# First block's gate stored by itself, layers' vectors turned in front of the latent rows' attention, and three feed-forward norms modulated in rows

## The chip, the cores and the metric

The kernel runs on one core of one Trainium2 chip. The metric is the time of one execution on the device, in microseconds (us). PE is the matrix engine (TensorE), DVE VectorE, ACT ScalarE, POOL GpSimd and SP SyncE, which here only issues the weight loads.

## The reference

A first block and two layers of a second block, on 256 latent tokens and 256 context tokens of width 1024. What the change touches is modulation by vectors that come out of the condition `c`, and the gates:

```python
# first block
x = x + gate2[:, None, :] * y2            # y2: the retrieval of experts ("peer")
return rms_norm(x, final_norm_w)
# second block, per layer l; x: latents, xc: context (not in the last layer)
x = x + gt_a * _rms(y, g_attn_post[l])                       # y: attention output @ w_out
hf = _rms(x, g_ffn_pre[l]) * (1.0 + sc_f) + sh_f
x = x + gt_f * _rms(_swiglu(hf, w_gate, w_up, w_down), g_ffn_post[l])
```

`mod = silu(c) @ w_ada + b_ada` gives the shifts, scales and gates, six vectors of 1024 for each block or layer and stream.

## The kernel before, in words

All engines walk one hand-written list of steps, `PLAN` (`make_plan`), and each emits its part of a step, so that list is the program order on PE, DVE, ACT and POOL alike. `weave(a, b)` mixes two lists by a table of costs. Every engine executes in order, so a wait holds up all that stands behind it on that engine. Streams are named (layer, stream, part): stream 0 is the latents, 1 the context, part "a" the attention and "f" the feed-forward.

Weights come in chunks of 128 x 1024 through a ring: SP loads a chunk into one of four buffers `RAW`, ACT copies its high part into one of three buffers `SPL` (`split_hi`), DVE subtracts to get the low part (`split_lo`), and PE multiplies high and low parts (three products each, `bk<-SPL,HH` and so on). A chunk's `SPL` buffer is free once PE has used it. Tokens' features are held turned (features on partitions) as a high and a low part, `HH`/`HL` for the latents and `HCH`/`HCL` for the context. Rows of `w_ada` ("ada" steps) go through the same ring and are multiplied and summed by DVE (L1189) into columns of `MOD`.

**Vectors.** The modulation vectors are columns (one feature per partition). A gate is applied to rows (tokens on partitions), so it has to lie in rows: step `vt` of layer 0 turns 104 columns of `MOD` (the first block's gate `MOD[:, 40:48]` and the layer's 96) and 64 of `AB` on PE, ACT copies them to `TMP`, POOL stores them to DRAM (`vec`, L738 and L739), and later loads them back, broadcast to all 128 partitions (`row_of`, L747, 512 KB each). In layer 0 the row of the first block's gate (`gB2`) is loaded in the same step `vt`, behind both stores; `vt` stands after the last modulation of layer 0 (`mods 0 f`), just in front of `peer_out`. The step `peer_out` (DVE: eight operations of 128x512) multiplies the four banks of the retrieval's output by that row and adds them to x; then come the final norm and layer 0's latents. Step `gB` loads a layer's gate row once its last attention output is there.

**Loads by POOL.** `c_in` loads x, the context, small rows and the final norm's weight while the first block still runs.

**Norm in front of a feed-forward** (`pre_steps`). `an_b` on DVE updates x (two operations of 128x1024, L1164), ACT squares the two halves with a sum. `norm_k` (DVE, L1161) makes the mean, POOL raises it to the power -1/2 (L680), `norm_b` on DVE refines it by three small operations and multiplies the rows by it (two L1159). `nT` then turns eight blocks of 128x128 for each half i of the tokens on PE (L1786), in two steps of four. For the first four of a half ACT applies scale and shift as per-partition vectors (4 operations), for the others DVE (4 operations, L1161); ACT makes the high part of the half (128x1024), DVE the low part (two of 128x1024 at the end). The first matmul of the feed-forward waits for all of it. For (0, 1, f) and for (1, 0, f) these steps stand alone in the list; those of (0, 0, f) are woven into the context's feed-forward (0, 1), whose output step `fo` (four operations 128x512 on DVE, four squares on ACT) stands between the last two turnings.

PE's results lie in eight banks, taken in rotations; `take` waits until the bank's former content is read.

## Time and profile before

| | |
|---|---|
| runs | 2423.24, 2421.45, 2420.80 us; median 2421.45 |
| the profiled execution, its own time | 2421.29 us |
| its span, first to last instruction | 2419.2 us |
| busy: PE / DVE / ACT / POOL | 2189.0 / 1721.2 / 1145.4 / 59.6 us |
| mean granted TensorE clock | 0.955 of full speed |

The span leaves 2.1 us of the execution's time outside. In a timeline a line gives the start in us, the length, the engine, the source line, the operation with what it writes and reads; `x4` means four instructions in a row, and `[9.51 <-DMA ...]` means that the engine stood idle for 9.51 us before it and what ended the wait. Many lines of the source are helpers: L1155 is any two-input operation of DVE, L798 and L800 any activation, L1780 any matmul, L1786 any turning.

### The profile page before, as it was taken

The numbers are of one execution on the slowest core, as the hardware profiler recorded it, in microseconds if no ns is written. First come the engines' busy times: TensorE is split into PE (matmuls) and PEld (weight loads), VectorE is DVE, ScalarE is ACT, GpSimd is POOL, SyncE is SP. The second block draws the span as 40 slices with busy tenths as digits, with TensorE's granted clock in tenths as the row PEclk, the third lists the DMA queues.
The fourth block names the chain that finished last, engine by engine and source line by source line (L and its number), as shares of the span: only waits on it lengthen the run. The fifth ranks groups of instructions, "written<-read, shape, count | busy, mean of one in ns | idle before, by whom it ended". The sixth has DMA issues, their size and how long they took to land.

```text
span 2419.2 us, 37731 instructions
## 1 busy us (share of the span) xinstructions
PE 2189.0 (90%) x14570; PEld 1954.7 (81%) x14570; DVE 1721.2 (71%) x3370; ACT 1145.4 (47%) x1945; POOL 59.6 (2%) x76
## 2 busy tenths in 40 slices
PE   3998799999999999989977989799989988997998
PEld 2987799999987778879855666799979978667997
DVE  5667678889987777788845676577776665665554
ACT  2643344555554444454444445444454445454444
POOL 1000000000000000000001000000000000000000
PEclk9999999999999999999978999899999999898999
DMA  8648646664467877777731120477767763104664
GB/s 283 199 145 275 202 145 197 200 219 136 149 193 259 274 258 247 272 230 246 258 102 40 54 69 18 133 242 250 244 208 254 253 192 120 60 1 123 187 187 131
DMA packets 139120, 438.80 MB, mean 181 GB/s; under 512 B 15553, under 2 KB 38369, under 8 KB 138432
## 3 DMA queue, kind: packets, MB, share of 16 engines
q1 hardware_dynamic: 109440, 396.93, 51.5%
q10 hardware_dynamic: 25776, 23.97, 2.9%
q0 software_dynamic: 3728, 15.50, 1.8%
q8 instruction: 117, 1.92, 0.3%
q14 instruction: 59, 0.48, 0.1%
HBM read 422.58 MB, written 13.76 MB: 180 GB/s over the span
## 4 chain that ended last, share of the span: by engine, by line
PE 49%; DVE 13%; issue 10%; DMA 10%; ACT 5%; POOL 0%; ACTq 0%; DVEq 0%; POOLq 0%; SPq 0%
PE bk L1780 46%; DMA TMP<-kept 4%; DVE SPL L1155 4%; DMA RAW<-in_peer 3%; PE bk L1786 3%; ACT SPL L798 2%; DMA kept<-TMP 1%; DVE RAW L1189 1%; ACT R L800 1%; DVE R L1155 1%; DVE TMP L1155 1%; DVE ST L1170 1%; ACT R L798 1%; DVE R L1164 1%; DVE WHL L1155 1%
## 5 line engine op out<-in xcount | busy, mean ns | idle before, releaser
L1155 DVE TENSOR_TENSOR SPL<-RAW,SPL 128x1024 fp32r<-128x1024 f32 (+1 forms) x614 | 744.2, 1218 | 352.0 <-ACT SPL L798 350.6
L798 ACT ACTIVATE SPL<-RAW 128x1024 fp32r<-128x1024 f32 (+1 forms) x614 | 645.1, 1054 | 615.0 <-PE bk L1780 284.2
L1780 PE MATMUL bk<-HH,SPL 128*128 128x256 f32 x3840 | 748.6, 289 | 28.2 <-DVE HL L1155 13.7
L1780 PEld LDWEIGHTS bk<-HH,SPL 128*128 128x128 f32 x3840 | 622.4, 194 | 35.1 <-DVE HL L1155 14.3
L1780 PE MATMUL bk<-SPL,WHL 128*128 128x512 f32 x2328 | 553.8, 391 | 13.4 <-DVE WHL L1155 9.2
L1780 PE MATMUL bk<-HL,SPL 128*128 128x256 f32 x1920 | 547.9, 285 | 0.0
L1780 PEld LDWEIGHTS bk<-SPL,WHL 128*128 128x128 f32 x2328 | 428.5, 188 | 106.5 <-issue 19.2
L1780 PEld LDWEIGHTS bk<-HL,SPL 128*128 128x128 f32 x1920 | 373.4, 194 | 2.5
L1780 PE MATMUL bk<-SPL,HH 128*128 128x256 f32 (+1 forms) x1664 | 314.0, 291 | 31.4 <-DVE SPL L1155 19.4
L1780 PEld LDWEIGHTS bk<-SPL,HH 128*128 128x128 f32 x1664 | 267.4, 198 | 41.1 <-issue 24.3
L798 ACT ACTIVATE R<-bk 128x256 f32<-128x256 f32 (+4 forms) x350 | 169.1, 498 | 222.2 <-PE bk L1780 197.0
L1780 PE MATMUL bk<-R 128*64 128x256 f32 (+8 forms) x944 | 246.3, 410 | 24.9 <-ACT R L798 11.6
L1780 PE MATMUL bk<-SPL,HL 128*128 128x256 f32 (+1 forms) x832 | 239.7, 288 | 0.0
L1780 PEld LDWEIGHTS bk<-R 128*64 128x64 f32 (+5 forms) x944 | 137.2, 178 | 98.7 <-issue 36.8
L1189 DVE CUSTOM_DVE_ANT_0 RAW<-RAW,TMP 128x1024 f32<-128x1024 f32 x144 | 174.8, 1221 | 14.5 <-ACT TMP L798 7.6
L1780 PEld LDWEIGHTS bk<-SPL,HL 128*128 128x128 f32 x832 | 164.5, 198 | 0.0
L1786 PE MATMUL bk<-cons,R 128*128 128x128 f32 (+1 forms) x626 | 106.1, 305 | 57.9 <-DVE R L1159 23.0
L1786 PEld LDWEIGHTS bk<-cons,R 128*128 128x128 f32 (+1 forms) x626 | 78.2, 153 | 96.3 <-issue 35.6
L800 ACT ACTIVATE R<-bk,ST 128x512 f32<-128x512 f32 (+1 forms) x120 | 74.0, 617 | 140.6 <-DVE ST L1159 139.6
L1780 PE MATMUL bk<-HCH,SPL 128*128 128x256 f32 x704 | 131.1, 285 | 6.7 <-DVE HCL L1155 4.5
L1780 PEld LDWEIGHTS bk<-HCH,SPL 128*128 128x128 f32 x704 | 112.3, 194 | 8.0 <-DVE HCL L1155 4.9
L1170 DVE TENSOR_REDUCE ST<-bk 128x1 f32<-128x512 f32 (+1 forms) x120 | 71.9, 599 | 54.1 <-PE bk L1780 53.9
(136 smaller groups left out, 1940.8 us busy)
## 6 DMA issues: line engine op xcount, KB each, us to landing
RAW<-in_peer SPq DMA_DIRECT2D x256, 512.0 KB, 4.7
RAW<-in_ada SPq DMA_DIRECT2D x144, 512.0 KB, 4.8
RAW<-in_ffn SPq DMA_DIRECT2D x132, 512.0 KB, 4.3
RAW<-in_win SPq DMA_DIRECT2D x96, 512.0 KB, 4.7
RAW<-in_ffd SPq DMA_DIRECT2D x66, 512.0 KB, 4.3
RAW<-in_wout SPq DMA_DIRECT2D x32, 512.0 KB, 5.0
kept<-TMP ACTq DMA_DIRECT2D x88, 128.0 KB, 3.3
TMP<-kept ACTq DMA_DIRECT2D x66, 128.0 KB, 5.6
```

Source lines behind the costliest of these rows:

```text
L798: ins = e.activation(out, in_, func, bias=bias, scale=scale)
L800: ins = e.activation(out, in_, func, bias=bias, scale=scale, accum_out=accum)
L1155: e.tensor_tensor(out, a, b, op).then_inc(*dve.up(*points))
L1164: e.scalar_tensor_tensor(out=out, in0=a, scalar=s, in1=b, op0=op0, op1=op1).then_inc(*dve.up(*points))
L1170: e.tensor_reduce(out, a, AX.X, op).then_inc(*dve.up(*points))
L1189: e.tensor_tensor_reduce(out=raw(n) if last else spare[n in in_ext], in0=raw(n), in1=c, scale=1.0, scalar=0.0, op0=ALU.mult, op1=ALU.add, ...
L1780: ins = e.matmul(out, lhsT, rhs, start=start, stop=stop, skip_group_check=True)
L1786: ins = e.transpose(b[0:rows, n * P:(n + 1) * P], a, ident)
```

## The change

It has three parts.

1. The first block's gate gets a step of its own, `("vt", "peer")`: 8 columns are turned, copied and stored right after `gB1`, before the first block's output projection. Its row is loaded at the head of `c_in` instead of behind layer 0's stores.
2. The steps `vt` of layers 0 and 1 stand in front of the latents' attention rows (units of the differential heads first) instead of at the end of the stage before. Layer 0's now turns 96 columns of `MOD`.
3. The norms (0, 0, f), (0, 1, f) and (1, 0, f) apply scale and shift in rows. `gB` of part "a" loads two more rows, A = (1 + scale) * weight and B = shift. `norm_k` multiplies x by A (two operations 128x1024, the first ahead of the wait for the sum of squares), `norm_b` makes x * r + B (two L1164-type operations in place of two L1159). `nT` then only copies each four turned blocks as high part (ACT, 128x512) and subtracts (DVE, 128x512). The squares' unused output goes to another buffer.

```diff
@@ -266,7 +266,7 @@
-    plan += fill + [("merge", 0), ("merge", 1)] + [("gB1", h) for h in range(2)]
+    plan += fill + [("merge", 0), ("merge", 1)] + [("gB1", h) for h in range(2)] + [("vt", "peer")]
@@ -316,7 +316,7 @@
-    peer += late + [("mods", 0, "f"), ("vt", 0)]
+    peer += late + [("mods", 0, "f")]
@@ -324,11 +324,11 @@
-    plan += weave(others, rows[:mla]) + weave(heads, rows[mla:gqa]) + rows[gqa:-16] + [("sil2", 1)] + rows[-16:]
+    plan += [("vt", 0)] + weave(others, rows[:mla]) + weave(heads, rows[mla:gqa]) + rows[gqa:-16] + [("sil2", 1)] + rows[-16:]
-    ffn = weave(ffn_steps(0, 0)[:-3], last[24:]) + [("mods", 1, "f"), ("vt", 1)]
+    ffn = weave(ffn_steps(0, 0)[:-3], last[24:]) + [("mods", 1, "f")]
@@ -336,7 +336,7 @@
-    plan += weave(others, rows[:mla]) + weave(heads, rows[mla:gqa]) + rows[gqa:]
+    plan += [("vt", 1)] + weave(others, rows[:mla]) + weave(heads, rows[mla:gqa]) + rows[gqa:]
@@ -425,13 +425,15 @@
-        turned_mod = {0: MOD[:, 40:144], 1: MOD[:, 144:192]}
+        ROWNORM = {(0, 0, "f"): 17088, (0, 1, "f"): 13188, (1, 0, "f"): 17088}
+        turned_mod = {"peer": MOD[:, 40:48], 0: MOD[:, 48:144], 1: MOD[:, 144:192]}
+        vec_at = {"peer": TMP[:, 1024:1152], 0: TMP[:, 2560:2688], 1: TMP[:, 2560:2688]}
-        VECS = {"peer": (0, 0)}
+        VECS = {"peer": (1, 160)}
-                VECS[(l, s, "f", "A")], VECS[(l, s, "f", "B")] = (l, 120 + 32 * s), (l, 48 * s + 24 + (0 if l else 8))
+                VECS[(l, s, "f", "A")], VECS[(l, s, "f", "B")] = (l, 120 + 32 * s), (l, 48 * s + 24)
@@ -623,6 +625,9 @@
+        for t, a in ROWNORM.items():
+            NORM[t]["Ar"], NORM[t]["Br"] = R[:, a:a + 1024], R[:, a + 1024:a + 2048]
@@ -694,7 +699,7 @@
-                    pool.wait_ge(T.at("out", ("dT", 0, 0)))
+                    pool.wait_ge(T.at("out", ("dT", 0, 0)), T.at("vm", 0), T.at("vec", 0))
@@ -734,15 +739,17 @@
             def turn_rows(l):
-                n, m = turned_mod[l].shape[1], turned_ab[l].shape[1]
-                e.dma_start(vec_d[l, 0:n, :], TMP[0:n, 2560:2688]).then_inc(*T.up(f"d_mod{l}", 16, [("vm", l)]))
+                n = turned_mod[l].shape[1]
+                if l == "peer":
+                    e.dma_start(vec_d[1, 160:168, :], vec_at[l][0:n, :]).then_inc(*T.up("d_peer", 16, [("vec", "peer")]))
+                    return
+                m = turned_ab[l].shape[1]
+                e.dma_start(vec_d[l, 0:n, :], vec_at[l][0:n, :]).then_inc(*T.up(f"d_mod{l}", 16, [("vm", l)]))
-                if l == 0:
-                    row_of("peer", gB2)
             def row_of(key, dst):
-                pool.wait_ge(T.at("vm", l), T.at("vec", l))
+                pool.wait_ge(*[T.at("vec", "peer")] if key == "peer" else [T.at("vm", l), T.at("vec", l)])
@@ -750,9 +757,13 @@
             def gB(l, s, k):
+                if k == "a":
+                    for n in ("A", "B"):
+                        row_of((l, s, "f", n), NORM[(l, s, "f")][n + "r"])
             def c_in():
+                row_of("peer", gB2)
@@ -842,6 +853,9 @@
             def nT(t, i, k):
+                if t in ROWNORM:
+                    turn_hi(("nT", t, i, k), H[n["s"]], i, k)
+                    return
@@ -996,9 +1010,12 @@
             def turn_rows(l):
-                key, n, m = ("vt", l), turned_mod[l].shape[1], turned_ab[l].shape[1]
+                key, n = ("vt", l), turned_mod[l].shape[1]
-                A(TMP[0:n, 2560:2688], ps(*key)[0:n, 0:P], ACT.Copy)
+                A(vec_at[l][0:n, :], ps(*key)[0:n, 0:P], ACT.Copy, ("out", key))
+                if l == "peer":
+                    return
+                m = turned_ab[l].shape[1]
@@ -1106,7 +1123,7 @@
             def an_b(l, s, k):
-                    A(v2(QS[(l, s)]["oY"], 2)[:, i, :], LX[s][:, i, :], ACT.Square, ("ssn", l, s, k),
+                    A(v2(QS[(l, s)]["junk"], 2)[:, i, :], LX[s][:, i, :], ACT.Square, ("ssn", l, s, k),
@@ -1201,11 +1218,11 @@
-            def turn_lo(key, Hs, i, k):
+            def turn_lo(key, Hs, i, k, *points):
-                   ALU.subtract, ("out", key))
+                   ALU.subtract, ("out", key), *points)
@@ -1292,8 +1309,16 @@
             def norm_k(t):
-                dve.wait_ge(T.at("ssn", l, s, "a") if k == "f" else T.at("ssn", l - 1, s, "f"))
-                mean_eps(ss_of(t)[0], D, "norm", t)
+                before = ("ssn", l, s, "a") if k == "f" else ("ssn", l - 1, s, "f")
+                n = NORM[t]
+                for i in range(2):
+                    if t in ROWNORM:
+                        if i == 0:
+                            dve.wait_ge(T.at("row", t + ("A",)), dve.own)
+                        tt(v2(n["xn"], 2)[:, i, :], n["x3"][:, i, :], n["Ar"], ALU.mult)
+                    if i == 0:
+                        dve.wait_ge(T.at(*before))
+                        mean_eps(ss_of(t)[0], D, "norm", t)
@@ -1302,10 +1327,17 @@
+                    elif t in ROWNORM:
+                        dve.wait_ge(T.at("row", t + ("B",)))
+                        x = v2(n["xn"], 2)[:, i, :]
+                        stt(x, x, r[:, i:i + 1], n["Br"], ALU.mult, ALU.add, ("xn", t, i))
             def nT(t, i, k):
+                if t in ROWNORM:
+                    turn_lo(("nT", t, i, k), H[NORM[t]["s"]], i, k, ("hT", t, i))
+                    return
@@ -1987,7 +2019,11 @@
             def turn_rows(l):
-                b = take(("vt", l), (6, 7))
+                b = take(("vt", l), MIX if l == "peer" else PROJ[(l, 0)])
+                if l == "peer":
+                    pe.wait_ge(T.at("A2"))
+                    e.transpose(b[0:8, 0:P], turned_mod[l], ident).then_inc(*pe.up(("full", ("vt", l))))
+                    return
```

POOL, first place, from the power of a norm just ahead of `c_in`, through `c_in` (`R<-xs` to `R<-in_rows`) and the steps that follow it, to the end of the old step `vt`; before:

```order
24 L680 TENSOR_TENSOR ST<-ST,cons 128x2
25 L676 DMA TMP<-in_rows 128x2048
26 L676 DMA R<-xs 128x2048
27 L676 DMA R<-in_ctx 128x2x1024
28 L676 DMA R<-in_rows 128x640
29 L676 DMA R<-in_rows 128x1024
30 L680 TENSOR_TENSOR ST<-ST,cons 128x2
31 L676 DMA R<-in_wkvb 128x512
32 L676 DMA R<-in_wqb 128x768
33 L738 DMA vec<-TMP 104x128
34 L739 DMA vec<-TMP 64x128
35 L747 DMA R<-vec 128x1024
```

and now:

```order
25 L685 TENSOR_TENSOR ST<-ST,cons 128x2
26 L681 DMA TMP<-in_rows 128x2048
27 L754 DMA R<-vec 128x1024
28 L681 DMA R<-xs 128x2048
29 L681 DMA R<-in_ctx 128x2x1024
30 L681 DMA R<-in_rows 128x640
31 L681 DMA R<-in_rows 128x1024
32 L685 TENSOR_TENSOR ST<-ST,cons 128x2
33 L681 DMA R<-in_wkvb 128x512
34 L681 DMA R<-in_wqb 128x768
35 L685 TENSOR_TENSOR ST<-ST,cons 128x2 x3
36 L685 TENSOR_TENSOR ST<-ST,cons 128x20
```

A row load (`R<-vec`) stands at the head of `c_in`, and the two stores and the load behind `R<-in_wqb` are gone.

POOL, second place, around the output projections of layer 0, before (the two `R<-vec` are the gates of the latents and of the context, in that order):

```order
43 L680 TENSOR_TENSOR ST<-ST,cons 128x20
44 L680 TENSOR_TENSOR ST<-ST,cons 128x8
45 L676 DMA TMP<-in_rows 128x2048
46 L747 DMA R<-vec 128x1024 x2
47 L680 TENSOR_TENSOR ST<-ST,cons 128x2 x2
```

and now, where the order of the six is gate, A and B of the latents, then gate, A and B of the context:

```order
44 L685 TENSOR_TENSOR ST<-ST,cons 128x20
45 L685 TENSOR_TENSOR ST<-ST,cons 128x8
46 L681 DMA TMP<-in_rows 128x2048
47 L754 DMA R<-vec 128x1024 x6
48 L685 TENSOR_TENSOR ST<-ST,cons 128x2 x2
```

The context's gate was the second row load and is the fourth.

DVE, from the update of x in layer 1's attention output to the first split of its feed-forward, before:

```order
2631 L1164 SCALAR_TENSOR_TENSOR R<-R,ST 128x1024 x2
2632 L1161 TENSOR_SCALAR ST<-ST 128x2
2633 L1155 TENSOR_TENSOR ST<-ST 128x2
2634 L1164 SCALAR_TENSOR_TENSOR ST<-ST 128x2 x2
2635 L1159 TENSOR_SCALAR R<-R,ST 128x1024 x2
2636 L1161 TENSOR_SCALAR R<-bk,AB,MOD 128x128 x8
2637 L1155 TENSOR_TENSOR HL<-R,HH 128x8x128 x2
2638 L1155 TENSOR_TENSOR SPL<-RAW,SPL 128x1024 x2
```

and now:

```order
2635 L1181 SCALAR_TENSOR_TENSOR R<-R,ST 128x1024 x2
2636 L1172 TENSOR_TENSOR R<-R 128x1024
2637 L1178 TENSOR_SCALAR ST<-ST 128x2
2638 L1172 TENSOR_TENSOR R<-R 128x1024
2639 L1172 TENSOR_TENSOR ST<-ST 128x2
2640 L1181 SCALAR_TENSOR_TENSOR ST<-ST 128x2 x2
2641 L1181 SCALAR_TENSOR_TENSOR R<-R,ST 128x1024 x2
2642 L1172 TENSOR_TENSOR HL<-bk,HH 128x4x128 x4
2643 L1172 TENSOR_TENSOR SPL<-RAW,SPL 128x1024 x2
```

Two products with a row are new, one on each side of the small operation for the mean; eight operations on 128x128 and two on 128x1024 have become four on 128x512.

## Rows read from the trace of the kernel before

**Rows 1.** The page, part 1: busy time, share of the span and instructions of each engine
```profile
PE 2189.0 (90%) x14570; PEld 1954.7 (81%) x14570; DVE 1721.2 (71%) x3370; ACT 1145.4 (47%) x1945; POOL 59.6 (2%) x76
```

**Rows 2.** Timeline, 1195 to 1232: start, length (us), engine, line, instruction, idle before
```profile
1208.16 2.98 PE L1780 MATMUL bk<-SPL,WHL 128*128 128x512 f32 x12 [1.27 <-DVE WHL L1155]
...
1211.06 0.24 DVE L1155 TENSOR_TENSOR AB<-MOD,cols 128x8 f32<-128x8 f32 x2
...
1220.81 0.69 DVE L1155 TENSOR_TENSOR R<-bk,R 128x512 f32<-128x512 f32 x1 [9.51 <-DMA R<-vec]
...
1216.68 0.57 POOL L747 DMA_DIRECT2D R<-vec  x1 [2.94 <-DMA vec<-TMP]
...
1230.03 1.22 PE L1780 MATMUL bk<-R 32*128 32x256 f32 x2 [4.36 <-ACT R L800]
```

**Rows 3.** Windows: busy time of each engine, granted clock, DMA share, GB/s
```profile
1229.00:1233.00 4.00, 2.97 (x10) 2.32 (x11) 1.89 (x8) 2.60 (x9) 0.00 (x0) 0.50 0.74 247
```

**Rows 4.** Timeline of four engines at the norm of (1, 0), 2203 to 2221
```profile
2206.17 2.48 DVE L1164 SCALAR_TENSOR_TENSOR R<-R,ST 128x1024 f32<-128x1024 f32 x2
...
2209.86 0.17 DVE L1161 TENSOR_SCALAR ST<-ST 128x2 f32<-128x2 f32 x1 [1.22 <-ACT R L800]
...
2210.11 0.70 POOL L680 TENSOR_TENSOR ST<-ST,cons 128x2 f32<-128x2 f32 x1 [4.57 <-DVE ST L1161]
...
2211.43 1.42 DVE L1159 TENSOR_SCALAR R<-R,ST 128x1024 f32<-128x1024 f32 x2
...
2212.24 3.83 PE L1786 MATMUL bk<-cons,R 128*128 128x128 f32 x16 [8.78 <-DVE R L1159]
...
2213.39 1.51 ACT L798 ACTIVATE R<-bk,MOD,AB 128x128 f32<-128x128 f32 x4 [3.56 <-PE bk L1786]
...
2220.56 0.58 PE L1780 MATMUL bk<-HH,SPL 128*128 128x256 f32 x1 [4.49 <-DVE HL L1155]
```

**Rows 5.** View by tile, HH: count, ns min/median/max, first and last start, forms
```profile
L798 ACT ACTIVATE HH<-bk x18: 382/385/599, 270.7 to 2179.3; 128x256 fp32r<-128x256 f32 x12, 128x512 fp32r<-128x512 f32 x6
...
L1155 DVE TENSOR_TENSOR HL<-bk,HH x18: 424/425/693, 271.3 to 2179.7; 128x256 fp32r<-128x256 f32 x12, 128x512 fp32r<-128x512 f32 x6
```

**Rows 6.** Timeline of POOL and DVE, 1270 to 1285 and 1430 to 1440
```profile
1275.27 4.44 POOL L680 TENSOR_TENSOR ST<-ST,cons 128x20 f32<-128x20 f32 x1 [6.77 <-DVE ST L1161]
...
1275.10 2.38 DVE L1155 TENSOR_TENSOR SPL<-RAW,SPL 128x1024 fp32r<-128x1024 f32 x2
...
1433.97 3.53 POOL L680 TENSOR_TENSOR ST<-ST,cons 128x20 f32<-128x20 f32 x1 [13.14 <-DVE ST L1161]
```

**Rows 7.** Timeline of PE, at the context's norm of layer 0
```profile
1562.62 0.58 PE L1780 MATMUL bk<-HCH,SPL 128*128 128x256 f32 x1 [4.49 <-DVE HCL L1155]
```

**Rows 8.** Timeline of PE and DVE at the latent's norm of layer 0, 1764 to 1784
```profile
1774.47 2.48 DVE L1155 TENSOR_TENSOR R<-bk,R 128x512 f32<-128x512 f32 x4
...
1781.38 0.58 PE L1780 MATMUL bk<-HH,SPL 128*128 128x256 f32 x1 [9.19 <-DVE HL L1155]
```

**Rows 9.** Timeline of DVE and PE inside the context's feed-forward
```profile
1725.47 0.42 DVE L1155 TENSOR_TENSOR WHL<-R,WHL 128x256 fp32r<-128x256 f32 x1
...
1728.56 2.88 PE L1780 MATMUL bk<-SPL,WHL 128*128 128x512 f32 x12
```

**Rows 10.** Timeline of ACT, before layer 0's last scaling
```profile
1975.18 0.43 ACT L798 ACTIVATE TMP<-bk 48x128 f32<-48x128 f32 x2 [3.71 <-PE bk L1993]
```

**Rows 11.** View of line 747, the row loads: DMA from issue to landing
```profile
DMA to landing us min/median/max: 3.9/4.0/5.8
```

**Rows 12.** Windows while the context's inputs load (columns as in rows 3)
```profile
1018.00:1022.00 4.00, 4.00 (x28) 3.64 (x27) 1.06 (x2) 1.15 (x2) 0.00 (x0) 1.00 1.02 374
```

**Rows 13.** Timeline of PE, behind those loads
```profile
1028.29 0.36 PE L1780 MATMUL bk<-HH,SPL 128*128 128x256 f32 x1 [2.56 <-DVE SPL L1155]
```

**Rows 14.** Timeline of DVE and PE at the output projections of layer 0
```profile
1522.68 0.69 DVE L1155 TENSOR_TENSOR R<-bk,R 128x512 f32<-128x512 f32 x1 [1.32 <-ACT R L800]
...
1527.37 0.40 PE L1780 MATMUL bk<-SPL,HCH 128*128 128x256 f32 x2
```

## The prediction

> **What bounds the kernel now.** The page's part 1 comes first: PE is busy for 2189 of 2419 us [rows 1], so time is won where PE stands still, and any other engine matters only where PE waits for it. The list of PE's idle gaps then names the places that the change touches. At the end of the first block DVE waits 9.51 us for the gate's row, and PE stands still behind it [rows 2]. In front of three feed-forwards PE waits for the low part of the normed tokens: 4.49 us for (1, 0) [rows 4], 4.49 us for (0, 1) [rows 7], and 9.19 us for (0, 0) [rows 8]. All else in the change moves work between queues, and I read the DMA windows and the rows of POOL and DVE at the new places for what may be late there. The profiled execution is 2421.29 us long, 2.1 us of it outside the span, and the median of the runs is 2421.45; I add the sum to 2421.3.
>
> **1. The gate's own step.** Before, two stores, the wait for them and the load stand behind the last modulation. The load was issued at 1216.68 and DVE went on 4.1 us later [rows 2]. The gate's columns of `MOD` are complete long before, and the new row is loaded in the stretch of [rows 12], some 190 us ahead of its use. DVE's 9.51 us disappear. What is late next: `peer_out` also needs the retrieval's last matmuls, which ended at 1208.16 + 2.98 = 1211.14, and stands behind the AB operations, which end at 1211.30 [rows 2]. So it starts at 1211.3 and not at 1220.8: −9.5. Behind it come the final norm and the first norm of the latents, a chain of latencies with nothing bound to a time of its own, so it moves as a whole.
>
> The clock bears on this. PE has long pauses behind the chain, the last 4.36 us before 1230.03 [rows 2], and the granted clock is 0.50 in 1229 to 1233 [rows 3], the lower level of 1.2 GHz. With DVE's wait gone, these pauses shrink by up to 8 us together; whether what is left of them still lets the clock fall no row shows. PE spent 4 us at half clock there, worth at most 2.0 us. I take half: −1.0 (bounds 0 and −2.0).
>
> **2. The norm of (1, 0).** Followed down the new order, from the update of x, which ends at 2206.17 + 2.48 = 2208.65 [rows 4]. The first product with A is an operation with two inputs of 128x1024; two such take 2.38 us [rows 6], so 1.2 each. It fits into the 1.22 us in which DVE waited for the sum of squares [rows 4]: nothing. The mean ends at 2210.1, then the second product runs until 2211.3 beside POOL's power. Before, the power took 0.70 us and the scaling began at 2211.43. The second product has two inputs from SBUF, and beside such operations POOL's power of 128x20 took 4.44 us where it took 3.53 us alone [rows 6]: 0.91 us more. I take this for the new place, so the power ends at 2211.7, three small operations of DVE add 0.6 to 0.7, and the first x * r + B ends at 2212.4 + 1.24 = 2213.6. (The update's two operations are of that form, 2.48 us for the pair, against 1.42 for the pair of L1159.) The second ends at 2214.85. PE turns sixteen blocks in 3.83 us [rows 4], so four take about 1 us. The fourth group of four needs the bank of the first, which ACT (0.60 us for 128x512) and DVE (0.69 us) empty [rows 5]; it is turned by 2217.4, and the same two operations behind it end at 2218.75. Before, PE started at 2220.56: −1.8. The gain is small because four operations of 1.5 us on ACT and a pair of 1.22 us on DVE go out of the end of the chain while 2.1 us go in ahead of it. Bounds: −0.8 if turnings or semaphores cost more, −3.3 if the power is not slowed and turnings run at full clock.
>
> The Trainium skill ("SBUF — State Buffer", section "Who interferes with whom") says that a DVE instruction with two SBUF inputs contends with a GpSimd instruction that reads SBUF, and whoever came first blocks the other. The 4.44 against 3.53 us agree with it; by the rule a product already running would hold the power back until it ends, and without it both norms of this kind would be 0.5 us shorter each and the sum −17.4.
>
> **3. The norm of (0, 1).** It has the same structure and the same 4.49 us wait [rows 7]: −1.8, bounds −0.8 and −3.3. A and B have landed by then: they are asked for at the output projections, some 40 us earlier [rows 7, 14].
>
> **4. The norm of (0, 0).** Its turnings lie in the context's feed-forward; only what follows the output step `fo` is exposed. DVE's four operations there ran from 1774.47 to 1776.95, then came 1.4 us of scaling, ACT's high part and 2.55 us of low part, and PE started at 1781.38 [rows 8]. Now ACT has lost four scalings and a high part ahead of `fo`, and a weight chunk's copy, hence `fo`, is about 1.1 us earlier. Squares end near 1775.9, then 0.60 of high part and 0.69 of low part [rows 5] give 1777.15: −4.2 (bounds −3 and −5). Against it: DVE gets two products (2.4 us) and 2 x 0.53 us more for x * r + B inside the feed-forward. PE reads the hidden part at 1728.56, whose low half was made at 1725.47 to 1725.9 [rows 9]; with 2.4 us in front this is 1728.3, just in time. I charge +0.5 for it (bounds 0 and +2).
>
> **5. The turning of the vectors.** Layer 1's two copies of ACT (0.43 us) stood in front of the output step [rows 10], and now stand among rows with slack: −0.4. Layer 0's now stand in front of rows and hold ACT for that time: +0.3; the new step for 8 columns +0.1.
>
> **6. The row at the head of `c_in`.** It puts 0.5 MB ahead of x, the context and the rest. DMA is saturated there, share 1.02 at 374 GB/s [rows 12], and weights share it; PE already stalls 2.56 us on a low part behind that stretch [rows 13]. 0.52 MB at that rate are 1.4 us. The bounds are 0 (the ring's depth takes it) and +2.6 (the stall doubles); I take +0.7, half of the transfer's time.
>
> **7. Six rows in a queue.** The gate of the context was the second row load and is now the fourth, behind A and B of the latents. DVE scales the context's projection at 1522.68, and PE needs the next chunk's low part, which stands behind it on DVE, at 1527.37 [rows 14]. A row takes 4.0 us from issue to landing, the slowest took 5.8 [rows 11]; that one is this second row, issued near 1516.5, which landed just ahead of the scaling. Two rows more, at 374 GB/s, are 2.8 us: landing near 1525.4, low part 1.9 us later at 1527.3, just in time. If each row costs its whole 4.0 us, the landing is 8 us later and PE waits some 7.3. I take +0.7 (bounds 0 and +7.3), near the lower end, since the second row came 1.8 us behind a lone one's 4.0, not 4.0 behind. The rows of A and B of the context land later still and are needed some 20 us later.
>
> **The sum:** −9.5 −1.0 −1.8 −1.8 −4.2 +0.5 −0.4 +0.3 +0.1 +0.7 +0.7 = −16.4; 2421.3 − 16.4 = 2404.9, so 2405.
>
> **The rivals.** *The DMA is the next wait:* the rows in step 7 land one by one at 4.0 us each (+6.6 on the sum) and the stall in step 6 doubles (+1.9): 2413.4. For it: the 5.8 us of [rows 11] and the share of 1.02. Against: one row is only 1.4 us of data. *The early gate is given back in half:* when the 9.5 us go, the other stream's work woven beside the chain, which hid in the wait, stands in its way; 2410 to 2413. For it: DVE works for both streams in one order. Against: [rows 2] show no operation between the AB pair and `peer_out`. *More comes:* the clock stays at 2.4 GHz behind the chain, the power is not slowed and the turnings run at full clock: 2396 to 2400. *The change doesn't do what it says:* DVE still waits at `peer_out`, for another source, and the norms' gain is eaten by the added products: 2417 to 2421. *Slower:* DVE waits in order for the context's gate behind two more rows, and the weights' low parts queue behind it; this costs what the rows take. It eats all 17 us left without step 7 when the row lands after about 1542.6, which needs some 6.7 us for each of the four rows from their issue at 1516, against 4.0 for a lone one; at 8 us each it lands near 1548 and the time is 2427. Only a DMA queue slowed by the weights would do that, and [rows 11] have no row above 5.8.
>
> **How the numbers follow.** The forecast (2400 to 2409) 0.60; the DMA next 0.14; gate given back in half 0.10; more 0.09; no gain 0.04; slower 0.03; all of them make 1.0. The range 2398 to 2414 takes in the first three cases and part of the fourth, and leaves out less than 2 in 10. It is no wider since the bounds of single terms hardly meet: the large ones are those of steps 2, 3 and 7. 0.2% is 4.8 us, about what a measurement of this kernel can tell from no change, so faster means below 2416.6: 0.60 + 0.14 + 0.10 + 0.09 = 0.93; same is the no-gain case, 0.04; slower 0.03.
>
> **What the new profile would show.** Step 1: no wait of DVE for `R<-vec` at `peer_out`, which follows the AB pair at once; a granted clock over 0.50 in the stretch behind. Steps 2 and 3: PE's wait before the feed-forward near 2.7 us, POOL's power near 1.6 us and not 0.70. Step 4: PE's wait near 5, no new gap of PE in the feed-forward before. Step 6: the stall behind `c_in` up to 5 us. Step 7: DVE's wait ended by `R<-vec` at the context's scaling, and PE's behind it under 1 us. The prediction is wrong if a wait of several us for another source stands in place of the 9.51, if a row needs more than 6 us, or if the feed-forward (0, 1) has gaps from DVE's added work.

## The result, and the profile after

The changed kernel takes 2404.09 us (median of 6 runs, 2402.75 to 2410.26) and the kernel before 2419.94 us (6 runs). The medians lie 15.9 us apart. The ratio, which here is that of the mean times, is 0.994, with a 95% interval of 0.9926 to 0.9955: 14.5 us less, between 10.9 and 17.9. The forecast was 2405, from 16.4 us less than 2421.3.

Page, part 1, of the changed kernel, beside [rows 1]:

```profile
PE 2178.2 (91%) x14571; PEld 1948.0 (81%) x14571; DVE 1722.4 (72%) x3358; ACT 1137.9 (47%) x1928; POOL 65.8 (3%) x83
```

**The gate.** Timelines of PE and DVE of the changed kernel, at the places of [rows 2] (start, length, engine, line, instruction, idle before it):

```profile
1212.95 2.98 PE L1812 MATMUL bk<-SPL,WHL 128*128 128x512 f32 x12 [1.23 <-DVE WHL L1172]
...
1215.85 0.24 DVE L1172 TENSOR_TENSOR AB<-MOD,cols 128x8 f32<-128x8 f32 x2
1216.22 0.69 DVE L1172 TENSOR_TENSOR R<-bk,R 128x512 f32<-128x512 f32 x1
...
1225.44 0.90 PE L1812 MATMUL bk<-R 32*128 32x256 f32 x2 [3.13 <-ACT R L811]
```

The wait of 9.51 us is gone. `peer_out` follows the AB pair at once, 0.1 us behind its end, and nothing takes the wait's place. PE's matmul on R stood at 1230.03 and stands at 1225.44, while the retrieval's last matmuls are 4.8 us later than before (1212.95 against 1208.16): 9.4 us gained between the two. The granted clock comes up sooner behind it, too. In the table below no time shows for it. In a window the columns are the length, the busy time of PE, PEld, DVE, ACT and POOL, the granted clock, the DMA share and GB/s:

```profile
1225.00:1229.00 4.00, 3.56 (x15) 3.02 (x15) 1.70 (x7) 2.94 (x9) 0.00 (x0) 0.60 0.62 223
```

The kernel before had 0.50 in the stretch that answers to it [rows 3].

**The loads of `c_in`.** The stall of 2.56 us [rows 13] is 2.49 us now, and a second wait for a low part stands ahead of it:

```profile
1027.84 2.98 PE L1812 MATMUL bk<-SPL,WHL 128*128 128x512 f32 x12 [0.91 <-DVE SPL L1172]
1033.32 0.36 PE L1812 MATMUL bk<-HH,SPL 128*128 128x256 f32 x1 [2.49 <-DVE SPL L1172]
```

**The norm of (1, 0).** The rows that answer to [rows 4], of DVE, POOL and PE:

```profile
2192.54 1.23 DVE L1172 TENSOR_TENSOR R<-R 128x1024 f32<-128x1024 f32 x1
...
2193.75 1.22 DVE L1172 TENSOR_TENSOR R<-R 128x1024 f32<-128x1024 f32 x1
...
2193.92 1.60 POOL L685 TENSOR_TENSOR ST<-ST,cons 128x2 f32<-128x2 f32 x1 [4.60 <-DVE ST L1178]
...
2196.15 2.48 DVE L1181 SCALAR_TENSOR_TENSOR R<-R,ST 128x1024 f32<-128x1024 f32 x2
...
2197.49 3.68 PE L1818 MATMUL bk<-cons,R 128*128 128x128 f32 x16 [10.24 <-DVE R L1181]
...
2202.58 0.58 PE L1812 MATMUL bk<-HH,SPL 128*128 128x256 f32 x1 [1.41 <-DVE HL L1172]
```

Two stretches have to be read, not the last wait alone. The turnings start later (10.24 us of idle before them against 8.78), and from the first turning to the first matmul of the feed-forward it is 5.09 us against 2220.56 - 2212.24 = 8.32: +1.46 - 3.23 = -1.77 us. POOL's power takes 1.60 us and not 0.70.

**The other two norms, and the context's gate.** PE ahead of the feed-forwards of (0, 1) and (0, 0), as in [rows 7] and [rows 8], and DVE and PE where [rows 14] show the output projections:

```profile
1522.63 0.69 DVE L1172 TENSOR_TENSOR R<-bk,R 128x512 f32<-128x512 f32 x1 [6.12 <-DMA R<-vec]
...
1524.60 0.47 PE L1812 MATMUL bk<-SPL,HCH 128*128 128x256 f32 x2 [1.92 <-ACT SPL L809]
...
1553.07 3.67 PE L1818 MATMUL bk<-cons,R 128*128 128x128 f32 x16 [10.24 <-DVE R L1181]
1558.16 0.39 PE L1812 MATMUL bk<-HCH,SPL 128*128 128x256 f32 x1 [1.41 <-DVE HCL L1172]
...
1767.21 0.58 PE L1812 MATMUL bk<-HH,SPL 128*128 128x256 f32 x1 [4.23 <-DVE HL L1172]
```

(0, 1) shows the same two waits as (1, 0), 10.24 and 1.41 us. The clock behind them differs: it is 1.00 in the feed-forward's first microseconds at (0, 1), and still 0.50 at (1, 0):

```profile
1558.00:1563.00 5.00, 4.84 (x40) 4.84 (x41) 1.89 (x3) 1.39 (x2) 0.00 (x0) 1.00 0.36 105
2203.00:2205.00 2.00, 2.00 (x11) 2.00 (x11) 1.00 (x1) 0.00 (x0) 0.00 (x0) 0.50 0.01 4
```

Ahead of (0, 0) PE waits 4.23 us and not 9.19. New is DVE's 6.12 us for the context's gate, with a stall of PE behind it. The view of the row loads says why, beside [rows 11]:

```profile
DMA to landing us min/median/max: 3.6/5.0/12.3
```

**Where the whole difference lies.** In the table the start of the same matmul is taken in the profiles of two kernels, and each entry says how much longer (+) or shorter (-) a stretch is than in the kernel before. Stretches are named by the kernel before's times. The labels are those of the experiments below.

| stretch | what is in it | changed | e10 | e1 | e2 | e3 | e4 | e5 | e6 | e7 | e8 | e9 |
|---|---|---|---|---|---|---|---|---|---|---|---|---|
| 0 to 960 | nothing of the change but one 8-column turning | +3.9 | -2.1 | -5.4 | -1.3 | -1.3 | -3.6 | -4.3 | -5.6 | -3.0 | -3.4 | -4.5 |
| 960 to 1205 | the row at the head of `c_in` | +0.9 | -0.4 | +1.4 | +3.3 | +3.3 | +2.8 | +5.0 | +3.0 | +2.7 | +2.3 | +2.3 |
| 1205 to 1232 | `peer_out` | -9.7 | -9.6 | -9.6 | -0.6 | -10.2 | -9.5 | -9.4 | -9.4 | -0.8 | -9.7 | -9.9 |
| 1232 to 1500 | layer 0's attention | +0.1 | -2.3 | -0.3 | -4.3 | -2.3 | +0.7 | -2.1 | -1.8 | -4.0 | +0.1 | +0.4 |
| 1500 to 1535 | the context's gate | +2.1 | +1.2 | 0.0 | +1.7 | 0.0 | +3.7 | +1.7 | 0.0 | 0.0 | 0.0 | 0.0 |
| 1535 to 1563 | norm (0, 1) | -1.8 | -1.7 | 0.0 | -1.8 | -1.8 | -2.1 | -2.3 | -1.8 | 0.0 | -1.9 | -2.6 |
| 1563 to 1700 | the matmuls behind it | -2.7 | -1.3 | 0.0 | -1.4 | -0.7 | -0.8 | -1.2 | -0.7 | -2.8 | -0.7 | -2.7 |
| 1700 to 1713 | inside feed-forward (0, 1) | -2.1 | -2.0 | -2.0 | -1.0 | +0.3 | -2.1 | -2.0 | -0.4 | -2.0 | -2.1 | -2.0 |
| 1713 to 1781 | its end, norm (0, 0) | -5.0 | -4.7 | 0.0 | -4.9 | -4.9 | -4.2 | -5.0 | 0.0 | 0.0 | -4.7 | -4.8 |
| 1781 to 1970 | feed-forward (0, 0) | -0.4 | -1.0 | -0.6 | -1.1 | +0.1 | -1.0 | -1.0 | -0.2 | -0.8 | -0.4 | -1.0 |
| 1970 to 1994 | layer 1's vectors gone from here | -0.7 | -0.5 | 0.0 | -0.4 | -0.4 | -0.4 | -0.8 | -0.4 | 0.0 | -0.8 | -0.7 |
| 1994 to 2180 | layer 1's attention | -0.9 | +0.9 | +0.5 | +1.2 | +1.8 | -1.1 | -0.7 | -0.9 | +3.5 | -0.8 | +1.2 |
| 2180 to 2220 | norm (1, 0) | -1.8 | -1.8 | 0.0 | -1.8 | -1.8 | -1.9 | -2.3 | -1.8 | 0.0 | -1.9 | -2.6 |
| 2220 to 2400 | the last feed-forward | -0.2 | +0.3 | +0.9 | -0.2 | +0.2 | -0.2 | 0.0 | -0.2 | +1.0 | -0.2 | -1.5 |

Some rows repeat to a few tenths of a us whenever the same edit is in the kernel, and are 0.0 when it isn't. They are the three norms, where only e4's (0, 0) stands apart with -4.2, and layer 1's vectors. Others move by 2 to 10 us among kernels that are alike there: the first 960 us range from -5.6 to +3.9. This is the scatter against which a change of 15 us is read, and why the total of one pair of profiles (-18.2 us) must not be explained to its last microsecond. The stretch 1700 to 1713 is a case: -2.1 us looks like a gain of the norms, but e1 and e7, whose norms are the old ones, show -2.0 as well. The totals are no finer: the intervals of all the ratios below overlap with the changed kernel's, so what is said of a single edit rests on its rows, each from one profiled execution.

### The profile page after: what moved, and what is told of

Same layout as the page of the kernel before. It is cut to its first block, busy times and chain, and to the rows that moved or that the text cites. A ratio compares the mean times of both kernels' runs of the same rounds, so it can differ in the third digit from the quotient of the medians.

```text
span 2401.0 us, 37699 instructions
## 1 busy us (share of the span) xinstructions
PE 2178.2 (91%) x14571; PEld 1948.0 (81%) x14571; DVE 1722.4 (72%) x3358; ACT 1137.9 (47%) x1928; POOL 65.8 (3%) x83
## 3 DMA queue, kind: packets, MB, share of 16 engines
q8 instruction: 117, 1.92, 0.3%
## 4 chain that ended last, share of the span: by engine, by line
PE 51%; DVE 13%; issue 10%; DMA 8%; ACT 4%; POOL 0%; ACTq 0%; DVEq 0%; POOLq 0%; SPq 0%
PE bk L1812 49%; DVE SPL L1172 3%; DMA TMP<-kept 3%; PE bk L1818 3%; DMA RAW<-in_peer 2%; ACT SPL L809 1%; DMA kept<-TMP 1%; DVE R L1172 1%; DVE RAW L1206 1%; ACT R L811 1%; DVE ST L1187 1%; DVE R L1181 1%; DVE TMP L1172 1%; DMA HID<-kept 1%; DVE EXT L1206 1%
## 5 line engine op out<-in xcount | busy, mean ns | idle before, releaser
L1812 PE MATMUL bk<-R 128*64 128x256 f32 (+8 forms) x944 | 239.9, 404 | 18.7 <-ACT R L809 11.6
```

Of the source, the lines that this page charges most:

```text
L1812: ins = e.matmul(out, lhsT, rhs, start=start, stop=stop, skip_group_check=True)
```

## The experiments

**e1: the gate alone.** The kernel before with the gate's own step:

```diff
-    plan += fill + [("merge", 0), ("merge", 1)] + [("gB1", h) for h in range(2)]
+    plan += fill + [("merge", 0), ("merge", 1)] + [("gB1", h) for h in range(2)] + [("vt", "peer")]
...
             def c_in():
                 pool.wait_ge(T.at("mul", ("peer", 99)), T.at("saved"))
+                row_of("peer", gB2)
...
-                if l == 0:
-                    row_of("peer", gB2)
```

> The kernel before with part 1 of the change alone: the gate has its own step and its row is loaded at the head of the context's inputs; vectors of the layers and norms are as before. Theory (the wait is paid once and nothing takes its place): the first matmul behind the long pause after the first block's last step comes 9.4 us earlier than before, counted from the matmuls just ahead of it, and nothing else moves, so the time is 9 to 10 us under before. Rival (the gain of the whole change in this stretch rests on the vectors' turning having left it too): 7 us or less, since the two copies and the 104-column turning still stand there. Clock: if shorter pauses alone keep it up, the stretch behind gives another 1 us.

Measured: 2410.28 us, ratio 0.9964 (0.9949 to 0.9979). Timeline of DVE, the AB pair and `peer_out`:

```profile
1207.04 0.24 DVE L1161 TENSOR_TENSOR AB<-MOD,cols 128x8 f32<-128x8 f32 x2
1207.41 0.69 DVE L1161 TENSOR_TENSOR R<-bk,R 128x512 f32<-128x512 f32 x1
```

The stretch of `peer_out` is 9.6 us shorter, and no row of the norms or of layer 1's vectors moves with it. The vectors' turning, which still stands there, costs nothing, so the rival falls. A gain by the clock in 1232 to 1500 does not show (-0.3). The whole is 8.7 us (5.1 to 12.3) where 9 to 10 were expected.

**e2: all but the gate.** The changed kernel, with layer 0's vectors and the gate turned and loaded at the old place:

```diff
-    peer += late + [("mods", 0, "f")]
+    peer += late + [("mods", 0, "f"), ("vt", 0)]
...
-    plan += [("vt", 0)] + weave(others, rows[:mla]) + weave(heads, rows[mla:gqa]) + rows[gqa:-16] + [("sil2", 1)] + rows[-16:]
+    plan += weave(others, rows[:mla]) + weave(heads, rows[mla:gqa]) + rows[gqa:-16] + [("sil2", 1)] + rows[-16:]
...
             def c_in():
-                row_of("peer", gB2)
```

> The changed kernel without part 1: layer 0's vectors and the gate are turned, stored and loaded where the kernel before does it, all else (the three norms in rows, layer 1's vectors at their new place) as changed. Theory: DVE waits 9.5 us for the row again and the time is 9 to 10 us over the changed kernel. What is left against before is what the norms give: by the sum of the prediction 7 us, by the two traces 13 us, since they show 6 us more behind the norms than the three waits account for. Rival (these 6 us were an accident of the one execution that was profiled): 7 us or less.

Measured: 2407.39 us, ratio 0.996 (0.9945 to 0.9975). DVE waits again:

```profile
1222.17 0.69 DVE L1173 TENSOR_TENSOR R<-bk,R 128x512 f32<-128x512 f32 x1 [8.94 <-DMA R<-vec]
```

The norms' rows of the table stand as in the changed kernel. The stretch 960 to 1205 is +3.3 without the early row, and -0.4 to +5.0 with it, so its total can't tell what the row at the head of `c_in` costs. PE's waits there can, in part. Ahead of the stall of 2.3 to 2.8 us that all kernels have, a wait of 0.9 to 1.5 us for a chunk's low part stands in seven of the nine profiles with the early row. The three without it show none, 0.34 and 0.42. A hundred us later this extra microsecond is lost in the scatter.

Expected was a time 9 to 10 us over the changed kernel's. By the ratios (0.996 and 0.994) it is about 5 over, though the 9 us are all there in the stretch of `peer_out`. Of the difference, 4 us lie in 1232 to 1500, where this kernel is shorter. Against the kernel before 9.7 us (6.0 to 13.3) are left for the norms, between the sum's 7 and the two traces' 13, and this decides for neither. By the ratios e1 and e2 give 8.7 and 9.7 us, which is more than the 14.5 of both, but within the intervals.

**e3: both gates first.** The changed kernel with another order of the six row loads:

```diff
                 row_of((l, s, k), QS[(l, s)]["gB"])
-                if k == "a":
-                    for n in ("A", "B"):
-                        row_of((l, s, "f", n), NORM[(l, s, "f")][n + "r"])
+                if k == "a" and (l, s) != (0, 0):
+                    for q in ((1, 0) if l == 0 else (0,)):
+                        for n in ("A", "B"):
+                            row_of((l, q, "f", n), NORM[(l, q, "f")][n + "r"])
```

> The changed kernel with the six row loads of layer 0 in another order: both gates first, then A and B of the context, then A and B of the latents. Theory (the context's gate is late because it is the fourth of six): DVE's wait of 6.12 us for it falls to about 1.3 and PE's stall of 1.92 us at the next chunk goes, so the output projections end 1.9 us earlier than in the changed kernel; A and B of the context still land before 1540, some 4 us ahead of the first product. Rival (six rows together saturate the queue whatever their order): the first product waits for A instead and the norm starts as late as now, 0 us.

Measured: 2398.3 us, ratio 0.9931 (0.9898 to 0.9964). Timeline of DVE at the context's scaling:

```profile
1512.96 0.69 DVE L1173 TENSOR_TENSOR R<-bk,R 128x512 f32<-128x512 f32 x1 [2.12 <-DMA R<-vec]
```

The wait falls from 6.12 to 2.12 us, and the stretch 1500 to 1535 from +2.1 to 0.0. The norm behind starts with the same 10.2 us of idle, so A is there in time. The rival falls: the order decides, not the number of rows. The ratio's interval is too wide to show the 2 us.

**e4: the second product behind the power.** The second half's product with A stands between the two x * r + B:

```diff
-                        tt(v2(n["xn"], 2)[:, i, :], n["x3"][:, i, :], n["Ar"], ALU.mult)
+                        if i == 0:
+                            tt(v2(n["xn"], 2)[:, i, :], n["x3"][:, i, :], n["Ar"], ALU.mult)
...
                         x = v2(n["xn"], 2)[:, i, :]
+                        if i == 1:
+                            tt(x, n["x3"][:, i, :], n["Ar"], ALU.mult)
+                            dve.wait_ge(dve.own)
```

> The changed kernel with the second half's product with A taken away from POOL's power: it stands between the first half's x * r + B and the second's. Theory (the two-input operation holds POOL back): the power takes 0.70 us and not 1.60 at all three norms, the first turning starts 0.9 us earlier; the second half's rows come 0.4 us later, so PE starts the feed-forward between 0.5 us earlier and 0.4 us later than in the changed kernel. Rival (the power is slow there for another reason, such as ACT or the DMA): it still takes 1.6 us, the first turning does not move and PE starts 1.2 us later. Total within 1.5 us of the changed kernel either way; the length of the power decides.

Measured: 2403.3 us, ratio 0.9945 (0.9926 to 0.9963). Timelines of POOL and PE at (1, 0):

```profile
2192.66 0.70 POOL L685 TENSOR_TENSOR ST<-ST,cons 128x2 f32<-128x2 f32 x1 [4.59 <-DVE ST L1178]
...
2195.32 1.97 PE L1822 MATMUL bk<-cons,R 128*128 128x128 f32 x8 [9.33 <-DVE R L1181]
2197.78 1.97 PE L1822 MATMUL bk<-cons,R 128*128 128x128 f32 x8 [0.48 <-DVE R L1181]
```

The power is back at 0.70 us: DVE's product beside it made the 1.60. The idle before the turnings falls by 0.91 us, and most of it is given back, since the second half comes later: norms (0, 1) and (1, 0) take 0.1 to 0.3 us less in the table. At (0, 0) the gain is 0.5 to 0.8 us smaller here than in the changed kernel (-4.2), but e8 and e9, which have the same edit, show -4.7 and -4.8.

**e5: PE kept at work in the pauses.** PE turns a constant 64 times ahead of the turnings of (0, 1, f) and (1, 0, f):

```diff
             def nT(t, i, k):
+                if t in WARM and (i, k) == (0, 0):
...
+                    for _ in range(WARM[t]):
+                        e.transpose(b[:, 0:P], ident, ident)
                 pe.wait_ge(T.at("xn", t, i), T.at("cons"))
```

> The changed kernel, where PE, in its 10.24 us pause ahead of the turnings of (0, 1, f) and of (1, 0, f), turns a constant 64 times into the bank that the first turnings will take; nothing reads the results. Theory (part of what the norms cost is TensorE's clock, which falls in the pause and comes back only in the feed-forward): the granted clock stays at 1.0 there, the sixteen turnings take about 2.6 us and not 3.68, and the matmuls behind no longer run their first 1.5 to 3 us at half rate; PE starts the feed-forward 0.5 to 1 us earlier and is 2 to 2.5 us ahead ten us later, at each of the two norms: 4 to 5 us in all. Rival (the clock has fallen for another reason, or the extra turnings only bring it down earlier): the 64 turnings take 15 us and delay the norm by 5 us, or the rows behind stay as they are, 0 us.

Measured: 2396.1 us, ratio 0.9925 (0.991 to 0.994). PE at (0, 1), and windows from there on:

```profile
1546.68 3.19 PE L1818 MATMUL bk<-cons,R 128*128 128x128 f32 x16 [3.24 <-DVE R L1181]
```

```profile
1543.00:1547.00 4.00, 0.76 (x8) 0.52 (x6) 3.31 (x7) 0.00 (x0) 2.13 (x2) 1.00 0.19 77
1547.00:1551.00 4.00, 2.78 (x16) 1.97 (x13) 3.27 (x5) 2.78 (x5) 0.00 (x0) 0.58 0.17 54
1551.00:1554.00 3.00, 2.72 (x12) 2.72 (x13) 1.45 (x2) 0.44 (x1) 0.00 (x0) 0.50 0.09 27
```

The clock did not stay up, it fell later: 1.00 through the constant's turnings, 0.58 behind the 3.24 us that were still idle, and 0.50 on the feed-forward's first matmuls. Half a microsecond is won at each norm. The expected 4 to 5 us did not come in the rows (by the ratios it is 2.6 to 3.6 us faster than the changed kernel, within the intervals). The rows suggest that the filling was too short, which e9 tests.

**e6: norm (0, 0) undone.**

```diff
-        ROWNORM = {(0, 0, "f"): 17088, (0, 1, "f"): 13188, (1, 0, "f"): 17088}
+        ROWNORM = {(0, 1, "f"): 13188, (1, 0, "f"): 17088}
...
-                        row_of((l, s, "f", n), NORM[(l, s, "f")][n + "r"])
+                        if (l, s, "f") in ROWNORM:
+                            row_of((l, s, "f", n), NORM[(l, s, "f")][n + "r"])
```

> The changed kernel with the norm (0, 0, f) as before: scale and shift behind the turnings, no products with A, and its two rows are not loaded, so four row loads stand in the queue and the context's gate is the second again. Theory 1 (the norm's own gain): PE waits about 9.2 us and not 4.23 ahead of that feed-forward, so 5 us come back, and no other gap of PE in the context's feed-forward changes, since DVE's extra work there had been covered. Theory 2 (the queue of row loads made the context's gate late): DVE's wait of 6.12 us for it is gone, which takes 2 us off, as in the run with both gates first. Rival to 2 (the gate is late because the weights fill the DMA there): the wait stays near 6 us. Together 3 us over the changed kernel.

Measured: 2400.57 us, ratio 0.9943 (0.9928 to 0.9958). DVE at the context's gate, and PE ahead of the feed-forward (0, 0):

```profile
1509.51 0.69 DVE L1173 TENSOR_TENSOR R<-bk,R 128x512 f32<-128x512 f32 x1 [1.99 <-DMA R<-vec]
```

```profile
1764.63 0.58 PE L1813 MATMUL bk<-HH,SPL 128*128 128x256 f32 x1 [9.13 <-DVE HL L1173]
```

Both theories hold in the rows: 5.0 us come back at (0, 0), and the 2.1 us at the context's gate go, since it is the second row again. The wait alone accounts for 4.9 of the 5.0 (9.13 against 4.23), so next to nothing is left for DVE's extra 3.5 us of work inside the feed-forward: it had been covered. Expected over the changed kernel were 3 us; the ratios cannot tell that.

**e7: the old pause filled.** The kernel before, with a constant turned 24 times behind the last turning of (0, 1, f):

```diff
                 columns(("nT", t, i, k), v2(NORM[t]["xn"], 2)[:, i, :], rotation)
+                if t == (0, 1, "f") and (i, k) == (1, 1):
...
+                    for _ in range(24):
+                        e.transpose(bk[b][:, 0:P], ident, ident)
```

> The kernel before, where PE turns a constant 24 times behind the last turning of (0, 1, f), in its 4.49 us wait for the low part. This tells whether the time that the changed kernel gained behind this norm (2.7 us in its profiled execution, 0.7 to 1.4 in others) comes from the shorter pause alone. Theory (in the kernel before the pause of 4.49 us lets the clock fall): the wait ends when it did, the clock stays up behind it, and the stretch to 1570 gets up to 2.9 us shorter without any change of the norm. Rival (the clock behind the norm falls with the long pause ahead of the turnings, whatever follows): nothing changes behind the wait.

Measured: 2415.15 us in its single run, beside a median of 2414.69 (2412.11 to 2421.51) of the kernel before. The total shows no gain: this profile is 3.5 us longer in layer 1's attention, where nothing was changed. Only the rows can answer. Windows, first of the kernel before (the wait ends at 1562.62, [rows 7]), then of this one (it ends at 1557.58, both 5 us earlier in its time):

```profile
1557.00:1563.00 6.00, 1.51 (x7) 1.09 (x6) 4.92 (x10) 4.46 (x7) 0.00 (x0) 0.78 0.01 3
1563.00:1568.00 5.00, 5.00 (x25) 5.00 (x25) 0.70 (x1) 0.00 (x0) 0.00 (x0) 0.50 0.36 105
```

```profile
1553.00:1557.00 4.00, 2.98 (x25) 2.74 (x23) 3.29 (x6) 3.91 (x7) 0.00 (x0) 0.94 0.00 0
1558.00:1563.00 5.00, 5.00 (x45) 5.00 (x44) 1.88 (x2) 1.06 (x1) 0.00 (x0) 1.00 0.35 105
```

In five microseconds behind the wait this kernel does 45 matmuls, and the kernel before 25. The norm is the same and ends as late, and the stretch behind it is 2.8 us shorter. So the kernel before pays for its pause twice, in the wait and in the clock behind it. The change shortens the wait at both norms. The clock's part it takes back only now and then: 0.7 to 2.7 us behind (0, 1), nothing behind (1, 0).

**e8: three edits together** (e3, e4 and e5).

```diff
+                    for q in ((1, 0) if l == 0 else (0,)):
...
+                            tt(x, n["x3"][:, i, :], n["Ar"], ALU.mult)
...
+                    for _ in range(WARM[t]):
```

> The changed kernel with three edits: both gates first in the queue of row loads, the second product behind POOL's power, and 64 turnings of a constant in the pauses of (0, 1, f) and (1, 0, f). If the three add up: -2 for the gate, -0.3 at each of two norms, -4 to -5 for the clock, so 6.5 to 7.5 us under the changed kernel, near 2397 where the kernel before takes 2417 (ratio 0.991 to 0.992). Rival (noise of the clock in the rest of the kernel hides it): the ratio cannot be told from the changed kernel's 0.994.

Measured: 2398.2 us, ratio 0.9936 (0.9922 to 0.9949), like e10's, over e5's 0.9925, and not apart from either. In the rows the gate's 2.1 us are gone and the clock is down behind both norms. The sum I expected took the clock's 4 to 5 us for given, and they had not come in e5.

**e9: the pauses filled further.** As e8, with 80 turnings:

```diff
-            WARM = {(0, 1, "f"): 64, (1, 0, "f"): 64}
+            WARM = {(0, 1, "f"): 80, (1, 0, "f"): 80}
```

> The three edits of the combined version again (both gates first, second product behind the power, turnings of a constant in the pauses of (0, 1, f) and (1, 0, f), whose results nothing reads), with 80 turnings in place of 64. With 64, at 0.109 us each, PE still stood for 2.34 us before the first real turning, and the granted clock fell there all the same. Theory (the pause that is left lets the clock fall): 80 leave 0.6 us, the clock stays at 1.0 in both norms, the first eight turnings take 1.0 us and not 2, PE starts each feed-forward 0.3 to 1 us earlier than in the combined version with 64 and runs at full rate from the start: 1.5 to 3 us in all. Rival (turning a constant does not count as work for the clock, or the 3.4 us between the last turning and the feed-forward suffice): the slow stretch stays, 0 us.

Measured: 2394.82 us (6 runs, 2393.23 to 2397.43), ratio 0.9916 (0.9899 to 0.9933), the lowest of all, though its interval overlaps with e5's and e8's. PE at (0, 1), and windows there and at (1, 0):

```profile
1543.20 1.09 PE L1823 MATMUL bk<-cons,R 128*128 128x128 f32 x8 [0.59 <-DVE R L1182]
1545.66 1.25 PE L1823 MATMUL bk<-cons,R 128*128 128x128 f32 x8 [1.36 <-DVE R L1182]
1548.32 0.38 PE L1817 MATMUL bk<-HCH,SPL 128*128 128x256 f32 x1 [1.41 <-DVE HCL L1173]
```

```profile
1545.00:1548.00 3.00, 1.25 (x8) 0.83 (x8) 2.82 (x5) 1.65 (x3) 0.00 (x0) 1.00 0.00 0
1548.00:1553.00 5.00, 4.68 (x39) 4.68 (x40) 1.89 (x3) 1.55 (x2) 0.00 (x0) 1.00 0.30 108
...
2191.00:2194.00 3.00, 1.57 (x10) 1.15 (x11) 2.56 (x5) 2.14 (x3) 0.00 (x0) 1.00 0.00 0
2194.00:2199.00 5.00, 5.00 (x44) 5.00 (x43) 2.10 (x2) 2.07 (x2) 0.00 (x0) 1.00 0.34 110
```

Eight turnings take 1.09 us and not 1.97 (e4). The clock is 1.00 in both norms and behind them, 0.7 us are won in each norm against e8, 2.0 behind (0, 1) and 1.3 behind (1, 0): 4.7 us in the rows for sixteen more turnings in each pause (3.4 by the medians, 4.8 by the ratios), where 1.5 to 3 were expected. One profile each stands behind this. At (0, 1) the changed kernel's first profile has the same -2.7 without any filling. Behind (1, 0) no kernel without the 80 turnings gains more than 0.2 us, so there the 1.3 us can be put down to the filling.

**e10: the changed kernel again**, beside e9, with no edit.

> The changed kernel once more, beside the fullest version on one chip, since runs of one kernel differ by several us and the gains of single edits are 1 to 3 us. By the traces so far the changed kernel should be at 0.993 to 0.994 of the kernel before, and its stretch up to the inputs of the context should lie between 5 us ahead of and 5 us behind the kernel before, whatever the change. If its first 960 us are again 4 to 5 us longer than in the kernel before, the change does cost time there, against my reading that this is scatter.

Measured: 2398.36 us (6 runs, 2395.94 to 2404.53), ratio 0.9936 (0.9917 to 0.9954). Its first 960 us are 2.1 us shorter than in the kernel before, where the first profile of the same kernel had +3.9. So that part of the first profile was scatter, and the change costs nothing there. The two ratios of this kernel, 0.994 and 0.9936, agree.

## Why the prediction was right

The time was 2404.1 where 2405 was forecast, by the case forecast, and most steps can be checked in the table (changed and e10):

| step | predicted | measured | runs |
|---|---|---|---|
| 1, the gate's wait | -9.5 | -9.6 to -9.7 | e1, e2 |
| 1, the clock behind it | -1.0 | none that shows | e1: -0.3 |
| 2, norm (1, 0) | -1.8 | -1.8 | e1, e4 |
| 3, norm (0, 1) | -1.8 | -1.7 to -1.8 | e1, e4 |
| 4, norm (0, 0), with DVE's extra work | -3.7 | -4.7 to -5.0 | e6 |
| 5, layer 1's vectors; layer 0's | -0.4; +0.4 | -0.5 to -0.7; none that shows | e1 |
| 6, the row in `c_in` | +0.7 | a wait of about 1 in most profiles, not told from scatter in the time | e2, e7 |
| 7, six rows in a queue | +0.7 | +1.2 to +2.1 | e3, e6 |
| not in the sum: the clock behind (0, 1) | 0 | -1.3 to -2.7 | e7, e9 |

**Steps 2 and 3** were right, and by their own way. The first turning was to start 1.36 us later than before and did so by 1.46; POOL's power was to take 1.6 us and took 1.60. e4 shows that this comes from DVE's product: 0.70 without it. In the rows of the changed kernel the product ends at 2194.97 and the power 0.55 us later, as if it did its work only then. The Trainium skill ("SBUF — State Buffer", section "Who interferes with whom") calls the port pair that DVE's second SBUF input and POOL share an exclusive lock, for which the order of issue decides who waits; these rows agree. But the estimate of 0.5 us off each norm if the power were free came only in part (0.1 to 0.3), since the product has to run somewhere.

Two signs were named wrongly. PE's last wait was to be 2.7 us and was 1.41. The start of the feed-forward was right; the wait before it is shorter since part of PE's idle time lies between the groups of turnings. And a row that needs more than 6 us was named as a sign that the prediction is wrong. It came: the gate's own took 9.7 us and the slowest 12.3. The sign was set too tight, since step 7 itself let the gate land more than 7 us after its issue. What the sign stood for, the rows holding up DVE, did happen, at a price within step 7's bounds.

**Step 4** was too small by 1 to 1.3 us. The +0.5 for DVE's products inside the feed-forward was not needed (e6). Of the rest, `fo`, which I had 1.1 us earlier, came 1.4 us earlier, and behind it ACT's high part started 0.6 us before `fo` had ended, so that PE went on 0.9 us behind `fo` and not 1.3.

**Step 7** was too small by 0.5 to 1.4 us (3.0 in e4), inside its bounds. The mechanism was as described, and e3 and e6 both remove it by making the gate the second row again. The size was off: I took 1.4 us per row from the rate, and the fourth row, issued about 1.6 us after the first at 1511.37, released DVE at 1522.63, 9.7 us later. Against a lone row's 4.0 that is 1.9 us for each of the three rows in front of it. The sum counted from the second row of the kernel before, which landed at 1516.7 + 5.8 = 1522.5. The changed kernel is 4.8 us earlier there and got its gate at 1522.6, so it came 4.9 us later in the program, 2.4 for each of the two rows put in front. The rival's 4.0 was further off. PE's stall behind the gate was to be under 1 us and was 1.92.

**Step 6** is not settled. PE's wait of 0.91 us ahead of the old stall fits the +0.7, and 0.9 to 1.5 us show in most profiles with the row, but no time further on tells it from scatter.

**What the sum left out** is the granted clock behind the norms. Step 1 has a term for it (where none was found) and steps 2 to 4 have none. A pause of 4.49 us in front of a feed-forward made its first matmuls run at 0.50, and e7 shows what that costs: 2.8 us, with the norm untouched. In the changed kernel part of it comes back: 0.7 to 2.7 us behind (0, 1), different from one execution to the next, and nothing behind (1, 0), where the clock is still at 0.50 when the feed-forward starts.

That the time came out within 1 us is partly luck. The gain by the ratio is 14.5 us, not 16.4, and the kernel before, run beside the changed one, has a median of 2419.94, 1.4 us under the 2421.3 from which the sum started. Errors of single steps also offset each other: step 4 and the clock behind (0, 1) gave 2.3 to 4 us more than forecast, step 7 took 0.5 to 1.4 more and the clock behind the gate gave 1.0 less. The two ways of measuring do not quite meet, either. Without step 6, the terms of the table above add up to -19.6 us in the changed kernel's profile and -18.4 in e10's, and e1 and e2 together give 18.4 by their ratios; the two direct ratios say 14.5 us (10.9 to 17.9) and 15.5 (11.1 to 20.0). The sum of the prediction, 16.4, lies between. The kernel before's profile, to which all entries refer, is one execution, and a term that differs by 2 us among executions, as the clock's does, is no better known than that.

What stays open: these 3 to 4 us, why the stretch 1232 to 1500 varies by up to 3 us among kernels that are alike there and by up to 5 among all, and what moves the first 960 us. One rival of the prediction, that part of the early gate is given back, is not ruled out for that stretch: e2 and e7, with the late gate, have -4.3 and -4.0 there, the nine kernels with the early gate -0.8 on average. The kernel before's own profile, which has the late gate too and is the table's zero, speaks against it. No run decides this.

## What to carry to other kernels

A pause of TensorE can be paid twice, as the wait and as the slower matmuls behind it, as in e7, so a step that shortens a pause should be costed with the clock of the rows behind it. Where the wait cannot be removed, matmuls that nobody reads can fill it. In this kernel they paid in the rows when they left 0.6 us of the pause (e9) and little when they left 2.3 or 3.2 (e8, e5). When several loads join one queue, order them by when they are needed: two gates in front of four rows cost nothing, the same gate in the fourth place cost 1.2 to 3.7 us. And before the last microseconds of a difference are explained, lay several profiles side by side, stretch by stretch: what moves in kernels that don't have the edit isn't its effect.

## What the runs showed of the hardware

POOL's power of 128x2 takes 0.70 us alone and 1.60 us when DVE's product of two 128x1024 operands started 0.17 us ahead of it, and it ends 0.55 us after that product (changed kernel and e4).

64 turnings of a constant, which nobody reads, kept the granted clock at 1.00, which is the level of 2.4 GHz, in a pause where it otherwise was at 0.50; after the 3.24 us of idle behind them it fell to 0.50, 1.2 GHz (e5). With 80 turnings and 0.59 us of idle it stayed at 1.00, also through two further pauses of 1.36 and 1.41 us (e9). A turning of 128x128 took 0.11 to 0.14 us at the one level and 0.23 to 0.25 at the other.

Of six row loads of 0.5 MB, issued 0.53 us apart, the slowest took 12.3 us to land, where a lone one takes 4.0 (changed kernel; median of the kernel before).
